# Decode attention of a small YOCO trunk: eight key places, a maximum in two parts, another ACT order, query copies on GpSimd

## Chip, core and metric

The program runs on one core of one Trainium2 chip. The metric is the device time of one execution in microseconds. The kernel before takes 1780.01 us (median of three runs, 1779.8 to 1782.85).

PE is the matmul engine, ACT ScalarE, DVE VectorE, POOL GpSimd, SP the engine whose queue issues the loads and stores of this stage.

## The reference, cut to what matters

One inference step: an mLSTM layer, a shared key and value projection, a differential attention layer and a final norm, for 1024 prompt rows and for 8 decode batches of 4 rows each. The change touches the attention of the decode batches. Each has 8 pages of 128 past rows in a paged cache (chosen by `page_table`) and its 4 new rows:

```python
k_past = cache_k[page_table].reshape((db, past_len) + cache_k.shape[2:])
v_past = cache_v[page_table].reshape((db, past_len) + cache_v.shape[2:])
...
for kp, mk in zip(k_parts, masks):
    s = jnp.einsum('bqhcd,bkhcd->bhcqk', q, kp).astype(F32) * ATTN_SCALE
...
p = jax.nn.softmax(jnp.concatenate(scores, axis=-1), axis=-1)
w = p[:, :, 0] - lam * p[:, :, 1]
o = jnp.einsum('bhqk,bkhe->bqhe', w[..., start:start + s_len].astype(vp.dtype), vp)
```

There are 8 heads with two key parts (c) of 64 numbers each, so a batch has 8 x 2 x 4 = 64 rows of scores over 1056 columns (1024 past, 32 new of which the mask leaves the batch's own). Everything is fp32; the kernel splits an operand into a high part (rounded for the matmul) and a low part (the remainder) and adds the products.

## The kernel before

The decode stage is `decode_phase`, between the prompt's attention and the last output projection. It runs over `DB` = 8 batches, software-pipelined: body b works on the keys of batch b and the values of batch b−1 (and on PE, ACT and SP on what is left of batch b−2). Bodies 0, 1, 8 and 9 are written out, bodies 2 to 7 are a loop on each engine. Each engine runs its own fixed list of steps in order and meets the others at semaphores:

```python
PE_ORDER = ("T0", "V4", "V5", "T1", "V6", "T2", "V7", "N", "T3", "S0", "W", "S1",
            "T4", "V0", "T5", "V1", "T6", "V2", "T7", "S2", "V3", "S3")
ACT_ORDER = ("K0", "V0", "E", "K1", "Q", "X", "V1", "K2", "V2", "K3", "V3", "O", "W",
             "K4", "V4", "K5", "R0", "V5", "K6", "V6", "K7", "R1", "V7", "R2")
DVE_ORDER = ("K0", "K1", "E", "K2", "K3", "W", "K4", "K5", "R0", "K6", "K7", "R1", "R2", "M")
```

The steps, with the lines they have in the profile:

- **T p** (PE, L2545): transposes key page p, in two halves u = 2p and 2p+1 of four heads each, into one of three PSUM banks used in turn. Half u+3 needs the bank that half u had (with W taking one turn in the middle), so it waits until u was read by DVE.
- **K p**: ACT copies the high part of both halves (L2378), DVE writes the low part (L2468, inputs: a PSUM bank and the high part in SBUF).
- **Q** (ACT, L2399): four copies of 64 rows put this batch's query parts into the zeroed `QZ`, which the scores use as weights.
- **S g** (PE, L2559): 16 matmuls of `QZ` with 256 columns of keys (288 for S3). **R r**: ACT copies the rows of the low query part (L2390), DVE adds them to the others in `SR` (L2477).
- **M** (DVE): mask on the last 32 columns (L2483), maximum over 1056 columns (L2484), scaling (L2485). **E**: exponentials with their sum on ACT (L2404), reciprocal and product `cf = rc * sgn` on DVE (L2489, L2490). **X** (ACT, L2409): scales the rows by `cf`.
- **W**: PE transposes the weights (L2569, L2571), DVE adds the two parts (L2495, L2497), ACT writes the high part (L2414, L2415), DVE the low part (L2503, L2505, all operands in SBUF).
- **V p**: ACT copies value page p to its high part (L2385), GpSimd subtracts to get the low part (L2357, "value low"), PE does four matmuls (L2582). There are four places for value pages `VB`, four for the high and four for the low parts; ACT's copy of page p waits until PE is done with page p−4 in `av`.
- **N** (PE): the new rows' values. **O** (ACT): copies the output to `AVS`, which SP stores.

SP issues the loads in one fixed order: key pages 4 to 7 of batch b in turn with value pages 4 to 7 of batch b−1, a store, then key pages 0 to 3 of batch b+1 in turn with value pages 0 to 3 of batch b. A key page waits until the page four before it was transposed (four places, `KB`), a value page until the low of the page four before it is done. Behind the last value pages SP loads the eight tiles of y rows that the next stage adds to (`X1`, a view of the rows' buffer `Y_ROWS`).

Of the kernel before, what the change touches and what calls it, by code (L numbers as in the profile page):

```python
# [24 lines left out]
P = 128  # L25
# [3 lines left out]
NT = 8  # L29
# [95 lines left out]
def trunk_step(  # L125
# [50 lines left out]
    with ctx:  # L176
# [2041 lines left out]
        def decode_phase():  # L2218
# [3 lines left out]
            ROWS = H * 2 * DS  # L2222
            KB = RAW[:, 0:4 * D].rearrange("p (s n) -> p s n", s=4)
            VB = take(4, D)
            SR, SX = take(TOK), take(TOK)
            AVS = take(D)
            WS = take(NB * TS)
            sgn, mx, nm, sm, rc, cf = (take(1) for _ in range(6))
            QZ = WH[:, 0:H * 136]
# [8 lines left out]
            d_in, d_avs, d_yr = sem("d_in"), sem("d_avs"), sem("d_yr")  # L2238
            k_ld = [sem(f"d_k{s}") for s in range(4)]
            v_ld = [sem(f"d_v{s}") for s in range(4)]  # L2240
# [53 lines left out]
            with nc.Block() as block:  # L2294
                @block.sync
                def _(sp):
                    for j, dst in enumerate((VB[0:TS, 2, :], VB[0:TS, 3, :], AVS[0:TS, :])):
                        sp.dma_start(dst, d_smB[:, j, :]).then_inc(d_in, 16)

                    def keys(b, p):  # L2300

                        wait(sp, tp, 2 * PAGES * b + 2 * (p - 3))
                        src = cache_k[page(sp, b * PAGES + p), :, :, :, :]
                        sp.dma_start(KB[:, p % 4, :], src.rearrange("a p h c d -> (a p) (h c d)"))\
                          .then_inc(k_ld[p % 4], 16)

                    def values(i, p):

                        wait(sp, vl, PAGES * i + p - 3)
                        src = cache_v[page(sp, i * PAGES + p), :, :, :]  # L2310
                        sp.dma_start(VB[:, p % 4, :], src.rearrange("a p h e -> (a p) (h e)"))\
                          .then_inc(v_ld[p % 4], 16)

                    def store(i):
                        sp.wait_ge(avc, i + 1)
                        sp.dma_start(d_av[bass.ds(i, 1), :, :].rearrange("a r n -> (a r) n"), AVS[0:64, :])\
                          .then_inc(d_avs, 16)

                    def body(b):
                        for p in range(4, PAGES):  # L2320
                            keys(b, p)
                            values(b - 1, p)
                        if has_rest(b):
                            store(b - 2)
                        for p in range(4):
                            keys(b + 1, p)
                            values(b, p)

                    for p in range(PAGES):
                        keys(0, p)  # L2330
                    for p in range(4):
                        keys(1, p)
                        if p == 2:
                            sp.wait_ge(pre, 1)
                        values(0, p)
                    body(1)
                    with sp.Fori(2, DB - 1) as b:
                        body(b)
                    for p in range(4, PAGES):
                        keys(DB - 1, p)  # L2340
                        values(DB - 2, p)
                    store(DB - 3)
                    for p in range(PAGES):
                        values(DB - 1, p)
                    store(DB - 2)
                    for t in range(NT):
                        sp.dma_start(X1[:, t, :], d_y[tok(t, P), :]).then_inc(d_yr, 16)
                    store(DB - 1)
                    sp.wait_ge(d_avs, 16 * DB)
                    sp.wait_ge(d_yr, 16 * NT)  # L2350

                @block.gpsimd
                def _(pool):
                    with pool.Fori(0, DB) as i:
                        for p in range(PAGES):
                            pool.wait_ge(vh, PAGES * i + p + 1)
                            nc.gpsimd.tensor_tensor(VL[p % 4], VB[:, p % 4, :], VH[p % 4].bitcast(F32), ALU.subtract)\  # L2357
                              .then_inc(vl, 1)

                @block.scalar  # L2360
                def _(act):
# [10 lines left out]
                    def body(b):  # L2372
# [8 lines left out]
                        def v_high(p):  # L2381
                            act.wait_ge(v_ld[p % 4], 16 * (2 * i + p // 4 + 1))

                            wait(act, av, PAGES * i + p - 3)
                            act.activation(VH[p % 4], VB[:, p % 4, :], ACT.Copy).then_inc(vh, 1)  # L2385

# [4 lines left out]

                        def queries():

                            wait(act, sc, 4 * b)
                            for part, q in ((0, QH), (64, QL)):
                                for c in range(2):
                                    rows = slice(DK * c, DK * c + DK)
                                    at = part + DS * c
                                    act.activation(QZ.rearrange("p (h r) -> p h r", r=136)[rows, :, at:at + DS],  # L2399
                                                   q[rows, :, bass.ds(b * DS, DS)].bitcast(F32), ACT.Copy).then_inc(qz, 1)  # L2400

                        def exponentials():
                            act.wait_ge(mxs, i + 1)
                            act.activation(SR[0:64, :], SR[0:64, :], ACT.Exp, scale=ATTN_SCALE, bias=nm[0:64, :],  # L2404
                                           accum_out=sm[0:64, :]).then_inc(exd, 1)
# [18 lines left out]
                        for step in ACT_ORDER:  # L2424
                            if step[0] == "K" and has_keys(b):
                                k_high(int(step[1]))
                            elif step[0] == "R" and has_keys(b):
                                low_rows(int(step[1]))
                            elif step == "Q" and has_keys(b):
                                queries()  # L2430
# [13 lines left out]
                def _(dve):  # L2444
# [16 lines left out]
                    def body(b):  # L2461
# [9 lines left out]
                        def add_rows(r):  # L2471
                            if r == 0 and has_weights(b):
# [35 lines left out]
                        for step in DVE_ORDER:  # L2508
# [4 lines left out]
                            elif step == "M" and has_keys(b):  # L2513
                                maximum()
                            elif step == "E" and has_weights(b):
                                shares()
# [5 lines left out]
                def _(pe):  # L2522
# [9 lines left out]
                    def body(b):  # L2532
                        i = b - 1

                        def turn(p):
                            pe.wait_ge(k_ld[p % 4], 16 * (2 * b + p // 4 + 1))
                            for j in range(2):
# [6 lines left out]
                                for h in range(4):  # L2544
                                    x = nc.tensor.transpose(T_BANK[u][:, h * P:(h + 1) * P],  # L2545
                                                            KB[:, p % 4, (4 * j + h) * P:(4 * j + h + 1) * P], ident)
                                x.then_inc(tp, 1)
# [101 lines left out]
```

## Time and profile before

| | us |
|---|---|
| median of three runs | 1780.01 |
| profiled execution | 1779.63 |
| its span, first to last instruction | 1777.8 |
| decode: from the first T0 (1409.70) to the next stage's first matmul (1659.80) | 250.1 |
| first batch, T0 to T0 | 20.75 |
| second batch | 28.70 |
| third to eighth batch, each | 27.83 to 27.91 |
| from the last S3's end of PE's eighth batch to the next stage | 33.5 |

Over the whole span PE is busy 94%, its weight loads 77%, DVE 54%, ACT 47% and GpSimd 25%. Those shares mix stages with different limits: the decode stage is 14% of the span, and only it contains what the change touches. In it the page's slices show DMA at 0.8 to 0.9 (nearly the only place in the program where it is), and a busy share of PE below that of the rest.

How to read the rows further down: a timeline row has its start (us from the span's start), its length, the engine, the line, output and inputs, how many merged instructions it stands for, and in brackets how long the engine had been idle ahead of it and who ended that. The ends of matmul records are modelled, so a record often overlaps the next start.

### The profile page before, as it was taken

To read this page: it belongs to the slowest core of one execution; us is meant where nothing else is said; L and a number is where in the kernel's file an instruction comes from. 1 tells how busy PE (TensorE), PEld (TensorE's weight loads), DVE (VectorE), ACT (ScalarE), POOL (GpSimd) and SP (SyncE) were. 2 spreads that over 40 slices of the span, in tenths; PEclk is the share of its full clock that TensorE was granted. 3 is DMA by queue.
4 is the path that set the end of the run, shared out by engine and by line. 5 is a ranking of instruction groups with operands and counts; after the bars stand their busy time and mean duration, and the time that the engine had idled before them with its cause. 6 is when DMAs were issued, how large, how long until landed. Compare 5 with 4: busy or idle time off the path is not lost. (4 is left out here: it accounts for less than half of the span.)

```text
span 1777.8 us, 30961 instructions
## 1 busy us (share of the span) xinstructions
PE 1665.1 (94%) x9247; PEld 1360.5 (77%) x9247; DVE 967.9 (54%) x2551; ACT 839.3 (47%) x1991; POOL 436.0 (25%) x866
## 2 busy tenths in 40 slices
PE   6999999999999979979999999999999689997798
PEld 5788888888888857768878878788788667775576
DVE  4454444544445343345776767767766455555343
ACT  5444443434445222343555545555544478876322
POOL 2122121221212210010122221221222147676201
PEclk9999999999999989989999999999998899998899
DMA  6212404033040113422121221111101388896713
GB/s 198 73 19 81 98 0 98 14 83 78 19 98 2 38 35 124 131 80 71 34 67 44 59 59 41 56 46 55 41 13 36 113 295 302 308 317 235 243 55 117
DMA packets 170406, 172.34 MB, mean 97 GB/s; under 512 B 13030, under 2 KB 140390, under 8 KB 170310
## 3 DMA queue, kind: packets, MB, share of 16 engines
q1 hardware_dynamic: 170310, 171.18, 31.9%
q8 instruction: 45, 0.74, 0.2%
q14 instruction: 51, 0.42, 0.1%
HBM read 142.24 MB, written 28.91 MB: 96 GB/s over the span
## 5 line engine op out<-in xcount | busy, mean ns | idle before, releaser
L1137 PE MATMUL PS<-WH,XH 128*128 128x512 f32 x512 | 212.7, 415 | 0.2 <-issue 0.2
L1137 PE MATMUL PS<-WH,XL 128*128 128x512 f32 x512 | 201.9, 394 | 0.0
L1137 PE MATMUL PS<-WL,XH 128*128 128x512 f32 x512 | 201.9, 394 | 0.0
L1867 ACT ACTIVATE WORK<-PD,WORK 128x896 f32<-128x896 f32 (+7 forms) x128 | 95.0, 743 | 62.1 <-DVE WORK L2034 57.3
L2113 PE MATMUL PS<-W,XH 128*128 128x512 f32 x384 | 123.8, 403 | 0.0
L1137 PEld LDWEIGHTS PS<-WH,XL 128*128 128x128 f32 x512 | 96.2, 188 | 22.9
L1137 PEld LDWEIGHTS PS<-WH,XH 128*128 128x128 f32 x512 | 96.8, 189 | 20.4 <-issue 0.6
L1137 PEld LDWEIGHTS PS<-WL,XH 128*128 128x128 f32 x512 | 96.8, 189 | 17.1
L1931 POOL TENSOR_SCALAR WORK<-WORK 128x1 f32<-128x1 f32 x64 | 19.9, 312 | 363.6 <-ACT WORK L1901 363.6
L2357 POOL TENSOR_TENSOR WL<-WORK,WH 128x1024 fp32r<-128x1024 f32 x32 | 76.2, 2383 | 94.2 <-ACT WH L2385 93.2
L730 POOL TENSOR_SCALAR WORK<-WORK 128x1 f32<-128x1 f32 (+1 forms) x72 | 13.8, 191 | 345.0 <-ACT WORK L581 345.0
L2033 DVE TENSOR_REDUCE WORK<-PD 128x1 f32<-128x896 f32 (+7 forms) x128 | 96.4, 753 | 2.2
L2113 PE MATMUL PS<-WH,XH 128*128 128x512 f32 (+2 forms) x224 | 86.5, 386 | 3.2 <-ACT WH L1832 3.2
L2468 DVE TENSOR_TENSOR XL<-PS,XH 128x512 fp32r<-128x512 f32 x96 | 63.5, 686 | 43.6 <-ACT XH L2378 41.3
L872 DVE SCALAR_TENSOR_TENSOR WORK<-PS,WORK 128x128 f32<-128x128 f32 (+1 forms) x72 | 20.1, 278 | 117.8 <-PE PS L1163 115.5
L2113 PE MATMUL PS<-WH,XL 128*128 128x512 f32 (+2 forms) x224 | 83.0, 370 | 0.0
L2113 PE MATMUL PS<-WL,XH 128*128 128x512 f32 (+2 forms) x224 | 82.8, 370 | 0.0
L2113 PEld LDWEIGHTS PS<-W,XH 128*128 128x128 f32 x384 | 68.8, 188 | 14.9 <-issue 1.4
L2195 PEld LDWEIGHTS PS<-RAW 128*128 128x128 f32 x576 | 75.1, 195 | 6.5 <-issue 1.4
L2545 PE MATMUL PS<-cst,RAW 128*128 128x128 f32 x384 | 58.3, 283 | 23.2 <-DVE XL L2468 18.8
L2357 POOL TENSOR_TENSOR WL<-WORK,VH 128x1024 fp32r<-128x1024 f32 x32 | 76.3, 2400 | 8.5 <-ACT VH L2385 8.5
L2195 PE MATMUL PS<-RAW 128*128 128x128 f32 x576 | 76.5, 279 | 1.3 <-DVE WORK L2000 1.3
(384 smaller groups left out, 4570.6 us busy)
## 6 DMA issues: line engine op xcount, KB each, us to landing
RAW<-in_cache_k SPq DMA_DIRECT2D x64, 512.0 KB, 5.1
WORK<-in_cache_v SPq DMA_DIRECT2D x64, 512.0 KB, 4.6
RAW<-in_w_in_a SPq DMA_DIRECT2D x40, 512.0 KB, 8.5
out<-WORK SPq DMA_DIRECT2D x16, 512.0 KB, 3.0
out<-RAW SPq DMA_DIRECT2D x16, 512.0 KB, 3.2
RAW<-in_w_in_b SPq DMA_DIRECT2D x60, 128.0 KB, 2.3
RAW<-in_w_kv SPq DMA_DIRECT2D x56, 128.0 KB, 2.2
YX<-in_x_prompt SPq DMA_DIRECT2D x8, 512.0 KB, 5.6
```

The source lines that it names most:

```text
L730: links.link(g_.tensor_scalar(var[0:n, b:b + 1], ssq[0:n, b:b + 1], 4.0 / P, 16 * EPS, ALU.mult, ALU.add))
L872: v.scalar_tensor_tensor(AT[0:n, t % 2, 0:n], B_S[0:n, 0:n], K_SCALE, EX[0:n, t % 2, 0:n], ALU.mult, ALU.mult).then_inc(at, 1)
L1137: last = nc.tensor.matmul(bank, x[:, k, tok(t, P)], wkvoz(w)[:, k, :], start=(k == i == 0), stop=(k == KT - 1 and i == 2))
L1867: act.activation(PR[:, c, 0:n], S[c][:, 0:n], ACT.Exp, scale=ATTN_SCALE, bias=nm[:, c:c + 1], accum_out=sm[:, c:c + 1]).then_inc(ex, 1)
L1931: links.link(g.tensor_scalar(var[:, b:b + 1], ssq[:, b:b + 1], 1.0 / P, EPS, ALU.mult, ALU.add))
L2033: links.link(v.tensor_reduce(mx[:, c:c + 1], S[c][:, 0:n], AX, ALU.max, negate=True))
L2113: last = nc.tensor.matmul(out, x[:, k, at(NT - 1 - s)], w[:, k, cols], start=(k == i == 0), stop=(k == KT - 1 and i == 2))
L2195: x = nc.tensor.matmul(B_O, WT[:, kb, :], V[:, kb, :], start=(kb == 0), stop=(kb == t))
L2357: nc.gpsimd.tensor_tensor(VL[p % 4], VB[:, p % 4, :], VH[p % 4].bitcast(F32), ALU.subtract)\
L2468: v.tensor_tensor(XL[cols], T_BANK[2 * p + j].rearrange("p (h t) -> p h t", h=4), XH[cols].bitcast(F32), ALU.subtract).then_inc(kl, 1)
L2545: x = nc.tensor.transpose(T_BANK[u][:, h * P:(h + 1) * P], KB[:, p % 4, (4 * j + h) * P:(4 * j + h + 1) * P], ident)
```

## The change

1. Key pages get eight places: pages 0 to 3 stay in `RAW`, pages 4 to 7 go to tiles 4 to 7 of the rows' buffer `X1`, which is empty in this stage. Key page p of batch b+1 is issued at the turn in SP's order at which page p of batch b has been transposed. All of batch 0's keys are issued at once. Tiles 0 to 3 of y are loaded ahead of the last value pages of batch 6, tiles 4 to 7 after the last transpose.
2. The maximum is taken in two parts: a new step P (DVE, between R1 and R2) reduces the first 768 columns to `mp`; M reduces the last 288, and the scaling takes the smaller of the two negated maxima.
3. ACT's list changes: V0 goes behind E and K1; V1, V2 and V3 each go behind the key copies that followed them (V3 also behind O and W); Q is taken out.
4. The four query copies become `queries` on GpSimd, ahead of the value lows of the same turn; GpSimd's loop runs over batches 1 to 7, with the first queries and the last lows outside.

```diff
-            KB = RAW[:, 0:4 * D].rearrange("p (s n) -> p s n", s=4)
+            key_page = lambda p: RAW[:, p * D:(p + 1) * D] if p < 4 else X1[:, p, :]
...
-            ACT_ORDER = ("K0", "V0", "E", "K1", "Q", "X", "V1", "K2", "V2", "K3", "V3", "O", "W",
+            ACT_ORDER = ("K0", "E", "K1", "V0", "X", "K2", "V1", "K3", "V2", "O", "W", "V3",
                          "K4", "V4", "K5", "R0", "V5", "K6", "V6", "K7", "R1", "V7", "R2")
-            DVE_ORDER = ("K0", "K1", "E", "K2", "K3", "W", "K4", "K5", "R0", "K6", "K7", "R1", "R2", "M")
+            DVE_ORDER = ("K0", "K1", "E", "K2", "K3", "W", "K4", "K5", "R0", "K6", "K7", "R1", "P", "R2", "M")
...
                     def keys(b, p):
 
-                        wait(sp, tp, 2 * PAGES * b + 2 * (p - 3))
+                        wait(sp, tp, 2 * PAGES * (b - 1) + 2 * (p + 1))
...
                     def body(b):
-                        for p in range(4, PAGES):
-                            keys(b, p)
-                            values(b - 1, p)
+                        for p in range(4):
+                            keys(b + 1, p)
+                            values(b - 1, p + 4)
                         if has_rest(b):
                             store(b - 2)
                         for p in range(4):
-                            keys(b + 1, p)
+                            keys(b + 1, p + 4)
                             values(b, p)
...
+                    def queries(b):
+
+                        wait(pool, sc, 4 * b)
+                        apart(pool)
+                        for part, q in ((0, QH), (64, QL)):
+                            for c in range(2):
+                                rows = slice(DK * c, DK * c + DK)
+                                at = part + DS * c
+                                nc.gpsimd.tensor_copy(QZ.rearrange("p (h r) -> p h r", r=136)[rows, :, at:at + DS],
+                                                      q[rows, :, bass.ds(b * DS, DS)].bitcast(F32)).then_inc(qz, 1)
+                        pool.wait_ge(qz, 4 * b + 4)
...
+                    queries(0)
+                    with pool.Fori(1, DB) as b:
+                        queries(b)
+                        lows(b - 1)
+                    lows(DB - 1)
...
+                        def part_maximum():
+                            dve.wait_ge(add, 3 * b + 2)
+                            if has_weights(b):
+                                dve.wait_ge(mxs, 2 * (i + 1))
+                            v.tensor_reduce(mp[0:64, :], SR[0:64, 0:3 * G], AX, ALU.max, negate=True).then_inc(mxs, 1)
...
-                            links.link(v.tensor_reduce(mx[0:64, :], SR[0:64, :], AX, ALU.max, negate=True))
-                            v.tensor_scalar(nm[0:64, :], mx[0:64, :], ATTN_SCALE, None, ALU.mult).then_inc(mxs, 1)
+                            links.link(v.tensor_reduce(mx[0:64, :], SR[0:64, 3 * G:TOK], AX, ALU.max, negate=True))
+                            dve.wait_ge(mxs, 2 * b + 1)
+                            v.tensor_scalar(nm[0:64, :], mx[0:64, :], mp[0:64, :], ATTN_SCALE, ALU.min, ALU.mult).then_inc(mxs, 1)
```

ACT in the second batch's body, from K0 to the weights, before: K0, V0 (1024 columns), E (1056), K1, the four query copies, X (1056), V1, K2, V2.

```order
L2378 ACTIVATE XH<-PS 128x4x128 x2
L2385 ACTIVATE WH<-WORK 128x1024
L2404 ACTIVATE WORK<-WORK 64x1056
L2378 ACTIVATE XH<-PD 128x4x128
L2378 ACTIVATE XH<-PS 128x4x128
L2399 ACTIVATE WH<-WH 64x8x4 x2
L2399 ACTIVATE WH<-QL 64x8x4 x2
L2409 ACTIVATE WORK<-WORK 64x1056
L2385 ACTIVATE WH<-WORK 128x1024
L2378 ACTIVATE XH<-PS 128x4x128
L2378 ACTIVATE XH<-PD 128x4x128
L2385 ACTIVATE VH<-WORK 128x1024
```

The same place on ACT after (L2402 are the key copies, L2409 the value copies, L2418 is E, L2423 X, L2428 the weights' high part):

```order
L2402 ACTIVATE XH<-PS 128x4x128 x2
L2418 ACTIVATE WORK<-WORK 64x1056
L2402 ACTIVATE XH<-PD 128x4x128
L2402 ACTIVATE XH<-PS 128x4x128
L2409 ACTIVATE WH<-WORK 128x1024
L2423 ACTIVATE WORK<-WORK 64x1056
L2402 ACTIVATE XH<-PS 128x4x128
L2402 ACTIVATE XH<-PD 128x4x128
L2409 ACTIVATE WH<-WORK 128x1024
L2402 ACTIVATE XH<-PS 128x4x128 x2
L2409 ACTIVATE VH<-WORK 128x1024
L2428 ACTIVATE WH<-WORK 128x8x32
```

K2 now stands directly behind X, and the value copies one place later each; the last of the four is behind the weights.

GpSimd in its loop after, from the query copies (L2364) to the first two value lows (L2371); before, the loop held the lows alone.

```order
L2364 COPY WH<-WH 64x8x4
L2364 ISA
L2364 COPY WH<-WH 64x8x4
L2364 ISA
L2364 COPY WH<-QL 64x8x4
L2364 ISA
L2364 COPY WH<-QL 64x8x4
L2366 REGISTER_ALU
L2370 ISA
L2371 TENSOR_TENSOR WL<-WORK,WH 128x1024
L2370 REGISTER_ALU
L2371 TENSOR_TENSOR WL<-WORK,WH 128x1024
```

Four copies were added in front of the eight lows of a turn, and nothing moved among the lows.

## Rows read from the trace of the kernel before

**Rows 1.** Stretches: bounds, length, busy PE PEld DVE ACT POOL, clock, DMA, GB/s.

```profile
1430.45:1459.15 28.70, 22.36 (x155) 18.96 (x154) 14.79 (x28) 21.16 (x36) 17.31 (x8) 0.94 0.80 284
1514.89:1542.72 27.83, 25.58 (x176) 20.04 (x174) 16.11 (x28) 22.16 (x38) 18.98 (x9) 1.00 0.90 315
```

**Rows 2.** Timeline of PE in one batch of the loop.

```profile
1518.94 0.66 PE L2545 MATMUL PS<-cst,RAW 128*128 128x128 f32 x4 [0.74 <-DVE XL L2468]
...
1524.72 0.66 PE L2545 MATMUL PS<-cst,RAW 128*128 128x128 f32 x4 [0.74 <-DVE XL L2468]
1527.19 0.71 PE L2569 MATMUL PD<-cst,WORK 64*128 64x64 f32 x8
...
1531.10 0.42 PE L2582 MATMUL PD<-WH 128*64 128x512 f32 x1 [0.18 <-issue]
...
1536.47 1.44 PE L2545 MATMUL PS<-cst,RAW 128*128 128x128 f32 x8 [0.31 <-DMA RAW<-in_cache_k]
```

**Rows 3.** Timeline of DVE in the same batch.

```profile
1515.53 0.45 DVE L2477 TENSOR_TENSOR WORK<-PD,WORK 64x288 f32<-64x288 f32 x1 [2.69 <-ACT WORK L2390]
...
1516.52 1.25 DVE L2484 TENSOR_REDUCE WORK<-WORK 64x1 f32<-64x1056 f32 x1
...
1518.20 1.29 DVE L2468 TENSOR_TENSOR XL<-PS,XH 128x512 fp32r<-128x512 f32 x2 [0.25 <-issue]
...
1521.15 0.15 DVE L2490 TENSOR_TENSOR WORK<-WORK 64x1 f32<-64x1 f32 x1
...
1529.41 1.49 DVE L2503 TENSOR_TENSOR WH<-WORK,WH 128x256 fp32r<-128x256 f32 x1 [0.60 <-ACT WH L2415]
1530.82 0.17 DVE L2505 TENSOR_TENSOR WH<-WORK,WH 32x32 fp32r<-32x32 f32 x1
...
1536.51 0.69 DVE L2468 TENSOR_TENSOR XL<-PS,XH 128x512 fp32r<-128x512 f32 x1 [0.80 <-ACT XH L2378]
```

**Rows 4.** Timeline of ACT in the same batch.

```profile
1520.13 0.47 ACT L2399 ACTIVATE WH<-WH 64x32 fp32r x2
...
1521.34 1.18 ACT L2409 ACTIVATE WORK<-WORK 64x1056 f32<-64x1056 f32 x1 [0.24 <-DVE WORK L2490]
1522.42 1.04 ACT L2385 ACTIVATE WH<-WORK 128x1024 fp32r<-128x1024 f32 x1
1523.37 0.57 ACT L2378 ACTIVATE XH<-PS 128x512 fp32r<-128x512 f32 x1
...
1524.32 1.05 ACT L2385 ACTIVATE VH<-WORK 128x1024 fp32r<-128x1024 f32 x1
```

**Rows 5.** Timeline of POOL in the same batch: value lows 0 to 3.

```profile
1518.02 2.39 POOL L2357 TENSOR_TENSOR WL<-WORK,WH 128x1024 fp32r<-128x1024 f32 x1 [1.58 <-ACT WH L2385]
1523.54 2.38 POOL L2357 TENSOR_TENSOR WL<-WORK,WH 128x1024 fp32r<-128x1024 f32 x1 [3.13 <-ACT WH L2385]
1525.88 4.74 POOL L2357 TENSOR_TENSOR WL<-WORK,VH 128x1024 fp32r<-128x1024 f32 x2
```

**Rows 6.** Timeline of DVE in the prompt's attention: a reduction of 384 columns.

```profile
1381.80 0.56 DVE L2033 TENSOR_REDUCE WORK<-PD 128x1 f32<-128x384 f32 x1
```

**Rows 7.** Timeline of POOL in the prompt's attention: a small operation with two inputs.

```profile
1395.63 0.46 POOL L1956 TENSOR_TENSOR WORK<-WORK 128x128 f32<-128x128 f32 x1
```

**Rows 8.** Timelines of PE and DVE in the second batch.

```profile
1439.98 0.66 PE L2545 MATMUL PS<-cst,RAW 128*128 128x128 f32 x4 [2.89 <-DVE XL L2468]
...
1446.15 0.43 DVE L2503 TENSOR_TENSOR WH<-WORK,WH 128x256 fp32r<-128x256 f32 x1 [0.60 <-ACT WH L2415]
```

**Rows 9.** Timeline of DVE after the last score: the eighth batch's weights.

```profile
1636.59 1.56 DVE L2503 TENSOR_TENSOR WH<-WORK,WH 128x256 fp32r<-128x256 f32 x1 [2.66 <-ACT WH L2415]
1638.07 2.32 DVE L2505 TENSOR_TENSOR WH<-WORK,WH 32x32 fp32r<-32x32 f32 x1
```

**Rows 10.** Timeline of SP (key page 7's issue) and landing times of value pages (L2311).

```profile
1530.51 0.34 SPq L2304 DMA_DIRECT2D RAW<-in_cache_k  x1
...
DMA to landing us min/median/max: 3.4/4.6/6.9
```

More of the change, by code:

```diff
@@ L2222, in decode_phase @@
             ROWS = H * 2 * DS
-            KB = RAW[:, 0:4 * D].rearrange("p (s n) -> p s n", s=4)
+            key_page = lambda p: RAW[:, p * D:(p + 1) * D] if p < 4 else X1[:, p, :]
             VB = take(4, D)
+            value_page = lambda p: VB[:, p % 4, :]
             SR, SX = take(TOK), take(TOK)
@@ L2227, in decode_phase @@
             WS = take(NB * TS)
-            sgn, mx, nm, sm, rc, cf = (take(1) for _ in range(6))
+            sgn, mx, mp, nm, sm, rc, cf = (take(1) for _ in range(7))
             QZ = WH[:, 0:H * 136]
@@ L2238, in decode_phase @@
             d_in, d_avs, d_yr = sem("d_in"), sem("d_avs"), sem("d_yr")
-            k_ld = [sem(f"d_k{s}") for s in range(4)]
+            k_ld = [sem(f"d_k{s}") for s in range(PAGES)]
             v_ld = [sem(f"d_v{s}") for s in range(4)]
@@ L2310, in values @@
                         src = cache_v[page(sp, i * PAGES + p), :, :, :]
[L2311 to L2312 removed]
+                        sp.dma_start(value_page(p), src.rearrange("a p h e -> (a p) (h e)")).then_inc(v_ld[p % 4], 16)
                     def store(i):
@@ L2331, in _ @@
                     for p in range(4):
-                        keys(1, p)
                         if p == 2:
@@ L2335, in _ @@
                         values(0, p)
+                    for p in range(PAGES):
+                        keys(1, p)
                     body(1)
@@ L2338, in _ @@
                         body(b)
+                    for t in range(4):
+                        sp.dma_start(X1[:, t, :], d_y[tok(t, P), :]).then_inc(d_yr, 16)
                     for p in range(4, PAGES):
-                        keys(DB - 1, p)
                         values(DB - 2, p)
@@ L2344, in _ @@
                         values(DB - 1, p)
+                    sp.wait_ge(tp, 2 * PAGES * DB)
+                    for t in range(4, NT):
+                        sp.dma_start(X1[:, t, :], d_y[tok(t, P), :]).then_inc(d_yr, 16)
                     store(DB - 2)
-                    for t in range(NT):
-                        sp.dma_start(X1[:, t, :], d_y[tok(t, P), :]).then_inc(d_yr, 16)
                     store(DB - 1)
@@ L2353, in _, with lows @@
                 def _(pool):
-                    with pool.Fori(0, DB) as i:
+                    def queries(b):
[8 more added lines that the diff above has]
+                        pool.wait_ge(qz, 4 * b + 4)
+                    def lows(i):
                         for p in range(PAGES):
                             pool.wait_ge(vh, PAGES * i + p + 1)
-                            nc.gpsimd.tensor_tensor(VL[p % 4], VB[:, p % 4, :], VH[p % 4].bitcast(F32), ALU.subtract)\
+                            nc.gpsimd.tensor_tensor(VL[p % 4], value_page(p), VH[p % 4].bitcast(F32), ALU.subtract)\
                               .then_inc(vl, 1)
+                        pool.wait_ge(vl, PAGES * i + PAGES)
+                    pool.wait_ge(pre2, 1)
+                    pool.wait_ge(ini, 2)
+                    pool.wait_ge(vn, 2)
+                    queries(0)
[3 more added lines that the diff above has]
+                    lows(DB - 1)
                 @block.scalar
@@ L2384, in v_high @@
                             wait(act, av, PAGES * i + p - 3)
-                            act.activation(VH[p % 4], VB[:, p % 4, :], ACT.Copy).then_inc(vh, 1)
+                            act.activation(VH[p % 4], value_page(p), ACT.Copy).then_inc(vh, 1)
                         def low_rows(r):
@@ L2390, in low_rows @@
                             act.activation(SX[0:64, at:at + n], bank[64:128, 0:n], ACT.Copy).then_inc(slo, 1)
[L2392 to L2400, printed above, removed]
                         def exponentials():
-                            act.wait_ge(mxs, i + 1)
+                            act.wait_ge(mxs, 2 * (i + 1))
                             act.activation(SR[0:64, :], SR[0:64, :], ACT.Exp, scale=ATTN_SCALE, bias=nm[0:64, :],
@@ L2428, in body @@
                                 low_rows(int(step[1]))
-                            elif step == "Q" and has_keys(b):
-                                queries()
                             elif step == "E" and has_weights(b):
@@ L2514, in body @@
                                 maximum()
+                            elif step == "P" and has_keys(b):
+                                part_maximum()
                             elif step == "E" and has_weights(b):
@@ L2535, in turn @@
                         def turn(p):
-                            pe.wait_ge(k_ld[p % 4], 16 * (2 * b + p // 4 + 1))
+                            pe.wait_ge(k_ld[p], 16 * (b + 1))
                             for j in range(2):
```

5 lines of the change are left out of this document (2 added, 3 removed).

## Prediction, made before the kernel ran

> **What bounds the kernel now.** I read the table of stretches first [rows 1]. The decode stage handles eight batches, one after the other. From the third to the eighth a batch takes 27.83 to 27.84 us, from one T0 on PE to the next; one of the six equal rows stands there. PE is busy 25.58 us of it, DVE 16.11, ACT 22.16 and GpSimd 18.98, at a granted clock of 1.00, with DMA at 0.90. So no engine is full, and the 27.83 is a ring of waits. The PE timeline shows where PE stands still [rows 2]: 0.74 before the second half of T1, 0.74 before the second half of T3 (both for DVE's low halves of keys), 0.18 before V0, and 0.31 before T7 for a key page. Recorded ends overlap the next start, so the two 0.74 are about 0.9 from start to start. What ends these waits is read from DVE and ACT [rows 3, 4]:
>
> - T1's second half waits for the first key low of the batch, which starts at 1518.20. DVE is held until then by the maximum over 1056 columns, 1.25 us from 1516.52.
> - T3's second half waits for the key low of page 2, whose high half ACT starts at 1523.37. Ahead of it on ACT stand the query copies (1520.13), X (1521.34) and value page 1 (1522.42).
> - V0 waits for the weights' low halves on DVE (L2503, L2505). L2503 takes 1.49 us from 1529.41 and ends at 1530.90, just after GpSimd's pair of value lows that began at 1525.88 ends at 1530.62 [rows 5]. In the second batch, with GpSimd idle, the same instruction takes 0.43 [rows 8]. At the end of the stage L2505 takes 2.32 behind such a low [rows 9]. So a DVE operation with both inputs in SBUF stands still while a value low runs; key lows (one input in PSUM) don't.
>
> The Trainium skill, "SBUF — State Buffer", section "Who interferes with whom", calls this a lock on a port pair shared by the two engines, kept for a whole instruction and given to whichever starts first; 0.43 against 1.49 agrees.
>
> **Maximum in two parts.** The part over 768 columns runs between R1 and R2, where DVE waits for the last score anyway (the addition of R2 starts at 1515.53 after a wait of 2.69, in the same timeline [rows 3]), and it needs about 1 us: hidden. On the path 288 columns are left. Two reductions give the slope, 1.25 us for 1056 columns and 0.56 for 384 [rows 3, 6]: 0.69/672, so 288 cost about 0.46 and the path loses 0.79. Bounds: 0.69 (if it costs what 384 columns do) and 0.9 (proportional). Key low, exponentials (E) and X start 0.79 earlier. The 0.9 before T1's second half shrinks to about 0.1.
>
> **ACT order and query copies.** Now K2 follows X at once. From X's start, K2 comes 1.08 later (as value page 1 does now, 1522.42 − 1521.34), and T3's second half 1.35 after K2's start (1524.72 − 1523.37): 2.43 after X. X moves from 1521.34 to 1520.55, so that half starts at 1522.98 instead of 1524.72, **1.74 earlier**. PE's own work allows it: without both waits it would be there at about 1523.0 (1524.72 less twice 0.9, plus the 0.1 left at T1). W and everything behind it move along. The page-0 value copy (1.06) now stands between K1 and X, where the queries (0.97) stood, so it costs X nothing.
>
> The four query copies go to GpSimd. Nearest rows: 0.24 each on ACT (half of 0.47 [rows 4]), 0.46 for a larger operation with two inputs on GpSimd [rows 7]; so 1.0 to 1.8 us a batch, and I take 1.4. They lie between value low 7, which ends at 1516.44 (1.58 before 1518.02 [rows 5]), and value low 0, which now starts near 1520.5: 4 us of cover, and S0 needs them only later. Cost nothing; past 4 us each further us would delay value low 0, which PE needs only after W.
>
> **From W to V0.** Today 3.91 us (1527.19 to 1531.10 [rows 2]). Everything is now counted from X. The copy of value page 1 follows K2's two (0.95, 1523.37 to 1524.32), lasts 1.04, and its low begins 0.08 behind it: X + 1.08 + 0.95 + 1.04 + 0.08 = X + 3.15. Lows follow each other by 2.34 and last 2.38 [rows 5], so low 2 ends at X + 7.87. W is at X + 2.43 + 2.47 = X + 4.90 (1527.19 − 1524.72), and L2503 is ready 2.22 behind W as today, at X + 7.12. It is held by low 2 and ends at X + 8.15 (0.28 after the low, as now). L2505 starts 0.08 ahead of that end, at X + 8.07, and ends at X + 8.24. S1 and T4 on PE end about 3.5 behind W, at X + 8.4, so V0 comes about 3.57 behind W with no wait: **0.34 saved**. This needs L2505 to be there before value low 3. With V3 behind W on ACT, the copy of page 3 starts about 0.13 before L2503 is ready (ACT's records overlap by 0.1), lasts 1.05, and its low asks 0.08 later, at X + 8.12. The margin is 0.05 us, and it is the weakest step.
>
> **Eight key places.** The 0.31 at T7 is worth nothing by itself: T7's second half waits for the low of page 6, which runs from 1536.51 to 1537.20 [rows 3], whatever the page does. But page 7 is requested only at 1530.51 [rows 10], behind a value request. With T7 two us earlier, its lateness would eat the gain. The eight places are cover, not a term. On SP the keys keep their turns between value requests. The rows of y that are now loaded ahead of the last value pages take the turns of keys that no longer exist: nothing.
>
> **The value pages** are asked for when a low frees a place. Value low 0 moves from 1518.02 to about 1520.5, while the copies of pages 4 to 7 are wanted 2 us earlier. A value page lands 4.6 us after its issue in the median and 6.9 at most [rows 10]; by the walk page 6 keeps about 0.4 us of slack. Some of the gain may stay here.
>
> **The sum.** Per batch 1.74 + 0.34 = 2.08 by starts; by PE's recorded waits 0.74 + 0.74 + 0.18 = 1.66. I take 1.9, nearer to the starts, with something left for pages: six batches, 11.4. The second batch has no first wait to W's lock, but a recorded 2.89 us before T3's second half [rows 8]; K2 without value page 1 (0.95) and with the shorter maximum (0.79) saves 1.8. The first batch loses the query copies ahead of K2: 0.9. After the last score, E now precedes value low 0, so value low 1 queues behind it and L2505 waits behind one low fewer: L2505, at 1640.39 today [rows 9], comes about 2.2 earlier (bounds 0.4 and 2.3; the nearer is the walk, since L2503 comes 0.28 before the low that would decide it). Together 11.4 + 1.8 + 0.9 + 2.2 = 16.3. The profiled execution took 1779.63 (span 1777.8), 0.4 below the median of 1780.01: 1763.3 against it, **1763.7** as a median.
>
> **The rivals.**
>
> (a) *Value low 3 beats L2505.* If GpSimd asks first, L2505 ends with low 3, at about X + 10.52 instead of X + 8.24: 2.28 us later in each of seven batches, 16.0 in all, and everything is given back: about 1780. For it: a margin of 0.05, and at the end of the stage a waiting low did go ahead of L2505. Against: there it had long been waiting. 0.25.
>
> (b) *GpSimd wins both close races* (the case on the slow side). Value low 0 now starts right beside L2490 (cf = rc·sgn, two SBUF inputs), which releases X. L2490 starts 0.10 us before it: today 1521.15, while value page 0 copied in the queries' place would end at 1521.17 and its low start at 1521.25. If GpSimd's hold starts over 0.1 us ahead of its record, L2490 waits a whole low, 2.36, and L2505 loses as well: 4.64 × 7 = 32.5, so 1763.7 + 32.5 = 1796. Against: ACT needs still more time between K1 and the copy, which favours DVE. 0.12. L2490 alone lost gives 1763.7 + 16.5 = 1780, 0.05.
>
> By the Trainium skill's rule of that section, first come first served, neither race is lost and the forecast stands; no row here shows so close a pair.
>
> (c) *Pages of values are late.* If they land in 6 us instead of 4.6, V5 and V6 on ACT start about 1 us late, and half of each batch's gain goes: 1763.7 + 7 = 1771. 0.08. Here the order does what it says, but the ring closes through SP.
>
> **How the numbers follow.** My forecast has 0.50. Against no change, 0.2% (3.6 us, about what a measurement of this kernel can tell) is the bound. Faster: 0.50, (c) 0.08, and 0.05 of (a), whose time could end a little below, 0.63 in all. Same: 0.17 of (a) and the 0.05 of L2490 alone, 0.22. Slower: (b) 0.12 and 0.03 of (a), 0.15. The forecast's own range is 1759 to 1769: 2.08 in each batch and 2.3 at the end give 1762.5, and a second batch at full clock (0.94 now [rows 1]) about 1.3 less; 1.66, 0.4 and late pages give 1767 to 1769. The range reaches to (a), 1759 to 1781, and leaves out (b) and the tails.
>
> **What would show it.** Right: a batch of 25.8 to 26.2 us between T0s; no wait over 0.2 before the second halves of T1 and T3; the second weights' low (today L2505) at 0.17 us and the product behind the reciprocal (today L2490) at 0.15; GpSimd's query copies over before value low 0. Wrong: the second weights' low at over 2 us (a), that product as well (b), ACT's value copies waiting for DMA (c), or a batch that stays at 27.8 with PE waiting somewhere else.

## The result and the profile after

The changed kernel takes **1764.65 us** (median of four runs, 1763.86 to 1766.19) against 1780.6 for the kernel before, timed beside it: ratio 0.9909, 95% interval 0.9892 to 0.9927. The prediction was 1763.7. The profiled execution took 1764.56, 15.07 less than that of before. Decode itself became 16.7 us shorter (233.4 us from the first T0, at 1411.21, to the next stage's first matmul; 250.1 before). Of that, 1.5 us were lost again ahead of it: decode's first T0 came at 1409.70 before, behind stages that no part of the change touches.

The stretches of the kernel after (bounds, length, busy PE PEld DVE ACT POOL, clock, DMA, GB/s): first batch, second batch, one batch of the loop, and from the end of the loop to the next stage.

```profile
1411.21:1431.07 19.86, 18.06 (x128) 16.19 (x129) 12.32 (x19) 9.94 (x18) 0.64 (x4) 0.91 1.01 395
1431.07:1458.08 27.01, 22.34 (x156) 19.03 (x154) 15.02 (x29) 20.38 (x32) 18.18 (x12) 0.94 0.78 273
1509.78:1535.65 25.87, 25.03 (x175) 20.15 (x174) 15.91 (x29) 21.34 (x34) 19.94 (x13) 1.00 0.91 336
1613.29:1644.65 31.36, 17.18 (x68) 8.58 (x65) 5.33 (x10) 13.33 (x18) 20.42 (x9) 0.76 0.52 183
```

Against [rows 1] a loop batch fell from 27.83 to 25.87 while PE's busy time hardly moved (25.58 to 25.03): waits went, work did not. PE's timeline in that batch (start, length, engine, line, operation; in brackets the idle time ahead and who ended it):

```profile
1513.14 0.66 PE L2566 MATMUL PS<-cst,RAW 128*128 128x128 f32 x4
...
1517.51 1.16 PE L2566 MATMUL PS<-cst,RAW 128*128 128x128 f32 x8
...
1520.50 0.71 PE L2590 MATMUL PD<-cst,WORK 64*128 64x64 f32 x8
...
1523.98 0.47 PE L2603 MATMUL PD<-WH 128*64 128x512 f32 x1
...
1530.18 0.66 PE L2566 MATMUL PS<-cst,Y_ROWS 128*128 128x128 f32 x4 [0.66 <-DVE XL L2480]
```

The second halves of T1 (1513.14) and T3 (inside the group at 1517.51) have no wait; [rows 2] had 0.74 at each. W is the row at 1520.50, V0 the one at 1523.98. The wait for a key page at T7 is gone too, but T7's second half (1530.18) waits 0.66 for page 6's key low. DVE in the same batch (L2502 is the shorter reduction, L2504 the scaling, L2480 key lows, L2509 `cf`, L2522 and L2524 the weights' lows):

```profile
1511.42 0.45 DVE L2502 TENSOR_REDUCE WORK<-WORK 64x1 f32<-64x288 f32 x1
1511.99 0.20 DVE L2504 TENSOR_SCALAR WORK<-WORK 64x1 f32<-64x1 f32 x1
1512.39 1.29 DVE L2480 TENSOR_TENSOR XL<-PS,XH 128x512 fp32r<-128x512 f32 x2 [0.20 <-issue]
...
1515.40 0.15 DVE L2509 TENSOR_TENSOR WORK<-WORK 64x1 f32<-64x1 f32 x1
...
1522.71 1.07 DVE L2522 TENSOR_TENSOR WH<-WORK,WH 128x256 fp32r<-128x256 f32 x1 [0.60 <-ACT WH L2429]
1523.71 0.17 DVE L2524 TENSOR_TENSOR WH<-WORK,WH 32x32 fp32r<-32x32 f32 x1
```

GpSimd: the first two rows are the query copies (two merged in each), the other four value lows 0 to 3.

```profile
1511.90 0.47 POOL L2364 CAST WH<-WH 64x32 fp32r x2 [0.55 <-POOL WL L2371]
1512.42 0.47 POOL L2364 CAST WH<-QL 64x32 fp32r x2
1515.49 2.39 POOL L2371 TENSOR_TENSOR WL<-WORK,WH 128x1024 fp32r<-128x1024 f32 x1 [2.60 <-ACT WH L2409]
1518.75 2.39 POOL L2371 TENSOR_TENSOR WL<-WORK,WH 128x1024 fp32r<-128x1024 f32 x1 [0.87 <-ACT WH L2409]
1521.10 2.41 POOL L2371 TENSOR_TENSOR WL<-WORK,VH 128x1024 fp32r<-128x1024 f32 x1
1523.71 2.44 POOL L2371 TENSOR_TENSOR WL<-WORK,VH 128x1024 fp32r<-128x1024 f32 x1 [0.20 <-ACT VH L2409]
```

The queries are over at 1512.89, 2.6 us before value low 0. L2522 stands still until value low 2 ends (1523.51), as [rows 3] showed for the same step. L2524 and value low 3 are recorded at the same hundredth, 1523.71, and L2524 takes 0.17. On ACT, X starts at 1515.59:

```profile
1515.59 1.18 ACT L2423 ACTIVATE WORK<-WORK 64x1056 f32<-64x1056 f32 x1 [0.17 <-DVE WORK L2509]
```

### The profile page after: what moved, and what is told of

The parts are those of the page before. It is cut to its first block and busy times, and to the rows that moved or that the text cites. A ratio compares the mean times of both kernels' runs of the same rounds, so it can differ in the third digit from the quotient of the medians.

```text
span 1762.7 us, 31001 instructions
## 1 busy us (share of the span) xinstructions
PE 1664.2 (94%) x9247; PEld 1362.8 (77%) x9247; DVE 965.6 (55%) x2559; ACT 832.8 (47%) x1959; POOL 442.9 (25%) x898
## 5 line engine op out<-in xcount | busy, mean ns | idle before, releaser
L2480 DVE TENSOR_TENSOR XL<-PS,XH 128x512 fp32r<-128x512 f32 x96 | 63.3, 687 | 39.1 <-ACT XH L2402 38.1
L2371 POOL TENSOR_TENSOR WL<-WORK,WH 128x1024 fp32r<-128x1024 f32 x32 | 76.2, 2385 | 32.0 <-ACT WH L2409 31.3
L2371 POOL TENSOR_TENSOR WL<-WORK,VH 128x1024 fp32r<-128x1024 f32 x32 | 76.9, 2406 | 11.5 <-ACT VH L2409 11.5
L668 ACT ACTIVATE WORK<-PS 128x512 f32<-128x512 f32 x64 | 38.2, 598 | 84.5 <-PE PS L1137 84.5
```

Source lines behind the costliest of these rows:

```text
L668: act.activation(PJS[:, t % 2, :, 0:2 * P], PJ[(3 + t) % 2].rearrange("p (a c) -> p a c", a=2), ACT.Copy).then_inc(ev, 1)
L2371: nc.gpsimd.tensor_tensor(VL[p % 4], value_page(p), VH[p % 4].bitcast(F32), ALU.subtract)\
L2480: v.tensor_tensor(XL[cols], T_BANK[2 * p + j].rearrange("p (h t) -> p h t", h=4), XH[cols].bitcast(F32), ALU.subtract).then_inc(kl, 1)
```

## The experiments

Decode lengths (first T0 to the next stage's first matmul) come from each profiled execution; a loop batch is the mean of five, from W to W. Ratios are to the kernel before, timed beside each, with the 95% interval. The other stages move by several us from run to run, so the decode columns are the cleaner measure. They are not free of PE's granted clock, whose mean over a stretch mixes its two levels, 1.2 and 2.4 GHz (a mean of 1.00 is the upper one throughout). In the loop it was 1.00, but for one of the five batches at 0.94, some 0.9 us longer, in each of three runs: four places, V3 ahead of O and W, and the tiny operation. Outside the loop it differed from run to run. The same kernel (R0 behind K6, both runs) took 26.55 us in its second batch at 0.87 and 25.44 at 1.00; PE's waits just ahead were alike (1.21 and 0.59), so why the clock fell in one of them is open.

| kernel | median us | ratio | decode | loop batch |
|---|---|---|---|---|
| before | 1780.01 | | 250.1 | 27.83 |
| changed | 1764.65 | 0.9909 [0.9892, 0.9927] | 233.4 | 25.87 |
| changed, again | 1765.88 | 0.9907 [0.9891, 0.9924] | 233.0 | 25.87 |
| eight places alone | 1781.38 | 0.9995 [0.9984, 1.0007] | 250.0 | 27.83 |
| changed, four places | 1777.27 | 0.9969 [0.9952, 0.9985] | 246.4 | 27.82 |
| changed, one maximum | 1770.89 | 0.9926 [0.9905, 0.9946] | 243.1 | 26.53 |
| changed, queries on ACT | 1771.6 | 0.9939 [0.9920, 0.9958] | 239.1 | 26.60 |
| changed, old ACT order | 1781.71 | 0.9995 [0.9986, 1.0005] | 250.2 | 27.67 |
| changed, V3 ahead of O and W | 1783.69 | 1.0007 [0.9996, 1.0017] | 252.5 | 28.16 |
| changed, tiny operation between the lows | 1778.55 | 0.9982 [0.9969, 0.9995] | 249.2 | 28.22 |
| changed, K6 ahead of V5 and R0 | 1762.19 | 0.9896 [0.9877, 0.9915] | 233.8 | 25.83 |
| changed, R0 behind K6 | 1761.34 | 0.9884 [0.9868, 0.9901] | 230.0 | 25.48 |
| the same, again | 1758.43 | 0.9869 [0.9848, 0.9889] | 228.8 | 25.51 |
| the same and V3 behind K4 | 1766.16 | 0.9914 [0.9898, 0.9929] | 236.5 | 26.41 |

**Eight places alone**, on the kernel before:

```diff
-            KB = RAW[:, 0:4 * D].rearrange("p (s n) -> p s n", s=4)
+            key_page = lambda p: RAW[:, p * D:(p + 1) * D] if p < 4 else X1[:, p, :]
...
-                        wait(sp, tp, 2 * PAGES * b + 2 * (p - 3))
+                        wait(sp, tp, 2 * PAGES * (b - 1) + 2 * (p + 1))
```

> The kernel before with the eight key places and SP's new order alone (one maximum, the old ACT order, queries on ACT). My account: the recorded 0.31 us wait for a key page before T7 goes away, but a batch stays at 27.8 us, since T7's second half waits for the low of page 6 anyway; the time stays within 0.1% of the kernel before (1780.6). Rival, the places as the source of a gain by themselves: 0.31 x 7 = 2.2 us off or more, a batch of 27.5 and about 1778.

No difference, and PE's timeline says why. The wait for page 7 is gone from T7, and its second half waits for DVE in its place:

```profile
1512.52 0.66 PE L2547 MATMUL PS<-cst,Y_ROWS 128*128 128x128 f32 x4 [0.66 <-DVE XL L2470]
```

**Changed, with four places** and the old order of loads (the reverse of the diff above):

> The changed kernel with four key places and the old order of loads; the rest as changed. My account: the places are cover for the gain. Page 7 is issued about 16 us after T0 (behind value page 6's request) and lands about 5.4 later, at 21.3, while T7 wants it at 19.1; T7's second half comes at about 21.8 instead of 20.4, so a batch is about 1.3 us longer (27.0 to 27.3) and the time about 1764.65 + 7 x 1.3 = 1774, with PE waiting for key pages by DMA before T6 and T7. Rival, the places do nothing: 1764.65 and 25.87.

12.6 us over the changed kernel, more than expected. PE waits for key pages, at other steps from batch to batch: 2.2 to 2.5 us in five of the six loop batches and 1.2 in the last. The batches lie between 27.4 and 28.0, and the one at the lower clock at 28.7:

```profile
1507.36 0.32 PE L2563 MATMUL PS<-cst,RAW 128*128 128x128 f32 x1 [2.40 <-DMA RAW<-in_cache_k]
...
1531.87 0.65 PE L2563 MATMUL PS<-cst,RAW 128*128 128x128 f32 x4 [1.46 <-DMA RAW<-in_cache_k]
```

So the places are worth nothing alone, and most of the gain hangs on them.

**Changed, with one maximum:**

```diff
-            DVE_ORDER = ("K0", "K1", "E", "K2", "K3", "W", "K4", "K5", "R0", "K6", "K7", "R1", "P", "R2", "M")
+            DVE_ORDER = ("K0", "K1", "E", "K2", "K3", "W", "K4", "K5", "R0", "K6", "K7", "R1", "R2", "M")
...
-                            links.link(v.tensor_reduce(mx[0:64, :], SR[0:64, 3 * G:TOK], AX, ALU.max, negate=True))
...
+                            links.link(v.tensor_reduce(mx[0:64, :], SR[0:64, :], AX, ALU.max, negate=True))
```

> The changed kernel with the maximum over 1056 columns in one piece (no step P). My account: it lies on the path from the last score to E, so E, X and all behind them come 0.8 us later; a batch is 26.6 to 26.7 us and the time about 1764.65 + 7 x 0.8 = 1770. Rival: it is hidden behind ACT's other work, 25.9 and 1765.

As expected: 0.66 us more in a batch, and the wait of [rows 2] before T1's second half is back with its 0.74:

```profile
1520.16 0.33 PE L2565 MATMUL PS<-cst,RAW 128*128 128x128 f32 x1 [0.74 <-DVE XL L2480]
```

The 243.1 in the table is more than the maximum's share: of the 9.7 us over the changed kernel 3.4 lie in the second batch, which ran at a lower clock here (0.78 against 0.94) with PE busy 26.04 us of it against 22.34:

```profile
1432.65:1463.01 30.36, 26.04 (x156) 22.41 (x155) 14.81 (x28) 20.39 (x32) 18.18 (x12) 0.78 0.69 236
```

**Changed, with the queries back on ACT** (GpSimd's copies taken out):

```diff
-            ACT_ORDER = ("K0", "E", "K1", "V0", "X", "K2", "V1", "K3", "V2", "O", "W", "V3",
+            ACT_ORDER = ("K0", "E", "K1", "Q", "V0", "X", "K2", "V1", "K3", "V2", "O", "W", "V3",
```

> The changed kernel with the four query copies back on ACT, between K1 and the copy of value page 0; GpSimd does value lows alone. My account: the copies push the copy of value page 0 and with it X by 0.69 us (1516.28 instead of 1515.59 in the fifth batch's terms), so a batch is about 26.6 us, the first batch loses 0.9, and the time is about 1764.65 + 7 x 0.69 + 0.9 = 1770.4. Rival, the copies on GpSimd are themselves in the way there (they hold the port at the maximum's steps): then taking them away gives some of that back and the time stays at 1765 to 1767.

As expected: 0.73 more in a batch. X and K2 come later, and T3's second half waits again:

```profile
1520.57 0.33 PE L2561 MATMUL PS<-cst,RAW 128*128 128x128 f32 x1 [0.58 <-DVE XL L2475]
```

**Changed, with ACT's old order** (without Q):

```diff
-            ACT_ORDER = ("K0", "E", "K1", "V0", "X", "K2", "V1", "K3", "V2", "O", "W", "V3",
+            ACT_ORDER = ("K0", "V0", "E", "K1", "X", "V1", "K2", "V2", "K3", "V3", "O", "W",
```

> The changed kernel with ACT's steps in the order before, without Q: K0 V0 E K1 X V1 K2 V2 K3 V3 O W; eight places, two-part maximum and queries on GpSimd stay. My account: V0 delays E by about 0.4 us, V1 ahead of K2 delays T3's second half by 0.95 more, and the weights' low is held by value low 3 as before the change (0.34): together 1.7 a batch, 27.5 us, and the time about 1764.65 + 7 x 1.7 = 1776.5. Rival (Q and the maximum carry the gain, the order little): 0.4 a batch, about 1767.5.

A miss in the total, 1781.71 for 1776.5. A loop batch comes out near the expected 27.5, with all but 0.16 of its gain lost; the rest lies in the second batch (2.2 us more, at a clock of 0.88 for 0.94) and in the tail (3.8), which the estimate counted together as one batch more. ACT's timeline (value page 0's copy, then E) and DVE's (the scaling, done at 1548.83):

```profile
1548.41 1.07 ACT L2409 ACTIVATE WH<-WORK 128x1024 fp32r<-128x1024 f32 x1 [0.27 <-PE PD L2603]
1549.38 1.16 ACT L2418 ACTIVATE WORK<-WORK 64x1056 f32<-64x1056 f32 x1
```

```profile
1548.63 0.20 DVE L2504 TENSOR_SCALAR WORK<-WORK 64x1 f32<-64x1 f32 x1
```

The maximum is ready at 1548.83, but E starts at 1549.38, behind V0, which had to wait for PE's products. In the kernel before V0 had ended just as the longer maximum did. So the shorter maximum brings E forward only with V0 out of its way, and K2 then still stands behind V1.

**Changed, with V3 ahead of O and W on ACT**, so that GpSimd asks for value low 3 early:

```diff
-            ACT_ORDER = ("K0", "E", "K1", "V0", "X", "K2", "V1", "K3", "V2", "O", "W", "V3",
+            ACT_ORDER = ("K0", "E", "K1", "V0", "X", "K2", "V1", "K3", "V2", "V3", "O", "W",
```

> The changed kernel with one step of ACT moved: V3 stands ahead of O and W again. My account (the port): value low 3 is then already waiting on GpSimd when value low 2 ends, so it goes ahead of the second weights' low (0.17 us now), which is held for a whole low, about 2.3 us, in six batches of the loop; V0 comes 2.2 later, a batch is about 28.1 us and the time about 1764.65 + 7 x 2.2 = 1780. Rival (no such hold between two lows; only ACT's order counts): the weights' high part starts 0.26 later behind V3, a batch is 26.1 and the time about 1766.5.

The whole gain is gone. DVE's timeline, and GpSimd's with value lows 2 and 3 back to back:

```profile
1521.68 0.85 DVE L2522 TENSOR_TENSOR WH<-WORK,WH 128x256 fp32r<-128x256 f32 x1 [0.81 <-ACT WH L2429]
1522.45 2.33 DVE L2524 TENSOR_TENSOR WH<-WORK,WH 32x32 fp32r<-32x32 f32 x1
```

```profile
1519.85 4.89 POOL L2371 TENSOR_TENSOR WL<-WORK,VH 128x1024 fp32r<-128x1024 f32 x2
```

L2524 takes 2.32 or 2.33 in all six loop batches: a low that already waits goes ahead of DVE's next operation.

**Changed, with one tiny DVE operation more** between the two lows of the weights, to move the close race alone:

```diff
+                            v.reciprocal(rc[0:64, :], sm[0:64, :])
                             v.tensor_tensor(WTS[0:TS, PAGES, TS:2 * TS], ws[0:TS, PAGES, :],
```

> The changed kernel with one tiny DVE operation more (the reciprocal of 64x1 once again, 0.14 to 0.18 us, one input) between the two weights' lows L2522 and L2524. In the changed kernel the recorded start of value low 3 on GpSimd and that of L2524 lie within 0.02 us of each other in every loop batch, and L2524 took 0.17. If the two race for a shared port and the first to ask is served for a whole instruction (theory): L2524 now asks some 0.17 us behind value low 3, takes 2.2 us instead of 0.17, a batch lasts about 28 us as in the kernel with V3 ahead of O and W, and the total is about 1780. If DVE wins because a short operation behind another of DVE is let through, whoever came first (rival): L2524 stays at 0.17, a batch at 25.9 to 26.05 us, and the total within 1.5 us of the changed kernel.

The theory holds. DVE's and GpSimd's timelines (L2525 is the second weights' low here):

```profile
1525.97 1.06 DVE L2522 TENSOR_TENSOR WH<-WORK,WH 128x256 fp32r<-128x256 f32 x1 [0.60 <-ACT WH L2429]
1526.95 0.15 DVE L2524 RECIPROCAL WORK<-WORK 64x1 f32<-64x1 f32 x1
1527.03 2.32 DVE L2525 TENSOR_TENSOR WH<-WORK,WH 32x32 fp32r<-32x32 f32 x1
```

```profile
1526.96 2.34 POOL L2371 TENSOR_TENSOR WL<-WORK,VH 128x1024 fp32r<-128x1024 f32 x1 [0.21 <-ACT VH L2409]
```

The second low now starts 0.07 behind value low 3 (0.06 to 0.10 in the six loop batches), takes 2.3 and with it the gain. In the eight traces of kernels without this edit that keep V3 between W and K4, the two starts lay within 0.02 of each other in 49 batches (all the loop's and one ahead of it), and DVE's operation took 0.17 in all of them. Whether a tie goes to DVE, or GpSimd asks a little later than its record says, is not shown.

**K6 earlier.** The wait that was left, T7's second half for page 6's low, was attacked in two ways on ACT (and R0 behind K6 on DVE in both). First K6 ahead of V5 and R0:

```diff
-                         "K4", "V4", "K5", "R0", "V5", "K6", "V6", "K7", "R1", "V7", "R2")
-            DVE_ORDER = ("K0", "K1", "E", "K2", "K3", "W", "K4", "K5", "R0", "K6", "K7", "R1", "P", "R2", "M")
+                         "K4", "V4", "K5", "K6", "V5", "R0", "V6", "K7", "R1", "V7", "R2")
+            DVE_ORDER = ("K0", "K1", "E", "K2", "K3", "W", "K4", "K5", "K6", "R0", "K7", "R1", "P", "R2", "M")
```

> The changed kernel with K6 ahead of V5 and R0 on ACT, and K6 ahead of R0 on DVE. In the changed kernel PE's one long wait left in a batch is 0.66 us before T7's second half, for the low of page 6, whose high half ACT starts at 1528.80 behind R0 and V5. My account: with K6 at about 1527.4 that wait goes, a batch is 25.2 us and the time about 1764.65 - 7 x 0.66 = 1760. Rival: the copy of value page 5 comes a microsecond later, its low and the next value pages with it, and the wait turns up again at V6, S3 or a value page: 25.7 to 26, no gain.

Short of what was expected: 25.6 to 25.7 in five of six batches, 26.44 in one. T7's wait is gone, but PE now waits 0.62 for page 7's low before S3, and in the long batch a value page was 1.41 late on ACT:

```profile
1528.87 0.40 PE L2580 MATMUL PD<-XH,WH 128*128 128x288 f32 x1 [0.62 <-DVE XL L2480]
```

```profile
1477.64 1.06 ACT L2409 ACTIVATE VH<-WORK 128x1024 fp32r<-128x1024 f32 x1 [1.41 <-DMA WORK<-in_cache_v]
```

Then only R0 behind K6 (on DVE as in the diff above):

```diff
-                         "K4", "V4", "K5", "R0", "V5", "K6", "V6", "K7", "R1", "V7", "R2")
+                         "K4", "V4", "K5", "V5", "K6", "R0", "V6", "K7", "R1", "V7", "R2")
```

> The same idea in a smaller step: only R0 goes behind K6 on ACT and DVE, V5 keeps its place ahead of K6. My account: K6 starts 0.5 us earlier, so the 0.66 before T7's second half shrinks to about 0.16; a batch is 25.4 us and the time about 1764.65 - 7 x 0.5 = 1761. Rival: V6 waits for its value page already (0.16 us for DMA in the fifth batch) and PE's gain is given back there or at S3: 25.7 or more.

As expected: 25.48 in a batch and 1761.34 in all. This kernel and the changed one were then run again beside each other:

> The changed kernel once more, on the same chip as the run with R0 behind K6 below, for a direct comparison. Both theories: as before, 1764.65 within 1.5 us, a batch of 25.87 us from one T0 to the next.

> The changed kernel with R0 moved behind K6 on ACT and DVE (V5, K6, R0 on ACT; K6, R0 on DVE), once more beside it. If the 0.66 us wait before T7's second half is the last thing that costs the loop (theory): the batches again 25.3 to 25.7 us against 25.87, some 0.4 us in each of six batches and at most 0.6 elsewhere, so 2 to 3.5 us under the changed kernel. If the 3.3 us between the two medians so far came from the chips' other stages (rival): within 1 us of it.

**This version beats both kernels**: 1758.43 beside 1765.88 for the changed one, decode 4.2 us shorter. In the loop it gains 0.36 to 0.39 a batch, as expected. The 7.5 between the medians is more than the expected 2 to 3.5. Of the 4.2 in decode 2.7 lie in the loop and 1.4 in the second batch, which ran at a clock of 1.00 here and of 0.94 in the changed kernel; the remaining 3.3 between the medians lie in other stages and weren't taken apart.

Last, the same with V3 behind K4, to take the race away:

```diff
-            ACT_ORDER = ("K0", "E", "K1", "V0", "X", "K2", "V1", "K3", "V2", "O", "W", "V3",
-                         "K4", "V4", "K5", "V5", "K6", "R0", "V6", "K7", "R1", "V7", "R2")
+            ACT_ORDER = ("K0", "E", "K1", "V0", "X", "K2", "V1", "K3", "V2", "O", "W", "K4",
+                         "V3", "V4", "K5", "V5", "K6", "R0", "V6", "K7", "R1", "V7", "R2")
```

> The changed kernel with R0 behind K6 (as in the two runs above) and V3 behind K4 on ACT, so that value low 3 asks some 2.2 us later and no longer within 0.02 us of L2524. If the close race costs nothing as long as DVE has it (theory): L2524 stays at 0.17, W to V0 at 3.5 us, and the batches as without this edit, 25.3 to 25.7 us; total 1757 to 1762. What speaks against (rival): value page 7 waits for the place that value low 3 frees, which now comes free at some 1528.3 instead of 1526.2 on the changed kernel's clock, lands 5.1 us later at 1533.4 and is copied at 1533.7; with any delay of the transfer V7 waits up to 1 us on ACT, and a batch lasts 26 to 26.5, the total 1762 to 1767.

The rival holds: value low 3 now comes 2.2 us behind L2524, but value page 7 comes late, and ACT waits for it in five of the six loop batches (0.94 to 1.29):

```profile
1504.66 1.06 ACT L2409 ACTIVATE VH<-WORK 128x1024 fp32r<-128x1024 f32 x1 [1.05 <-DMA WORK<-in_cache_v]
```

## Why the prediction was right, step by step

**The sum.** Predicted 0.9 + 1.8 + 11.4 + 2.2 = 16.3; measured by the stretches 0.89 (first batch), 1.69 (second), 11.9 (six batches: 2.08 once, 1.96 five times) and 2.17 (tail), together 16.6. (The third batch of the kernel before took 27.90, not 27.83, and the second batch's 1.8 is 0.95 + 0.79 = 1.74 rounded up; neither matters.) A loop batch gave 1.96 for the 1.9 taken, and that is in part luck: the 1.9 left 0.18 of the 2.08 for late value pages, which cost a batch next to nothing, while the maximum fell short by 0.16. That the median came within 1 us of the forecast is luck too, since the stages ahead of decode moved by 1.5.

**The maximum** was mis-sized. The reduction came out as worked out (0.45; the slope gave 0.46), but X comes 5.81 behind T0 after 6.45: 0.64, not 0.79. The reduction is 0.80 shorter, but the scaling starts 0.12 behind its end for 0.03, and E 0.24 behind the scaling's start for 0.18, as the scaling with a second scalar takes 0.20 for 0.14. The first half of the batch (T0 to W) gave 12.30 − 10.72 = 1.58 instead of 1.74.

**The walk from X** held to 0.1 us: value low 1 at X + 3.16 (3.15 predicted), W at 4.91 (4.90), the end of value low 2 at 7.92 (7.87), L2522 ready at 7.12 (7.12), L2524 at 8.12 (8.07), value low 3 at 8.12 (8.12). W to V0 took 3.48 for 3.91 and saved 0.43, more than the 0.34 of the sum. Behind V0 a batch is 0.05 longer than before, so 1.58 + 0.43 − 0.05 = 1.96.

**The close races.** L2509 stands 0.09 ahead of value low 0 (0.10 predicted) and takes 0.15: won. The margin of L2524, 0.05 by the walk, is 0.00 in the record. That DVE won was the least sure step, and the tiny operation shows that rival (a) was a real mechanism with the price put on it: 28.06 for 25.87 in most batches, 1778.55 in all (1780 predicted).

**The tail.** As walked, L2522 now starts ahead of the low that decides, and L2524 alone pays for it, one low earlier than in [rows 9]; DVE's timeline there, and GpSimd's from that low on:

```profile
1622.47 0.51 DVE L2522 TENSOR_TENSOR WH<-WORK,WH 128x256 fp32r<-128x256 f32 x1 [1.61 <-ACT WH L2429]
1622.91 2.31 DVE L2524 TENSOR_TENSOR WH<-WORK,WH 32x32 fp32r<-32x32 f32 x1
```

```profile
1622.66 4.85 POOL L2371 TENSOR_TENSOR WL<-WORK,VH 128x1024 fp32r<-128x1024 f32 x2
```

**Query copies** were over-priced (about 1 us for 1.4), which costs nothing, since they are hidden either way. **Key places**: "cover, not a term" is confirmed from both sides (0.9995 alone; 12.6 us without them). **Value pages**: ACT waits 0.16 to 0.17 for page 6 in two of the six loop batches, so its slack of 0.4 was used up there. The profile's list of DMA issues (output and input, queue, count, KB each, median us to landing) shows value pages landing later, 5.1 for 4.6 in [rows 10].

```profile
WORK<-in_cache_v SPq DMA_DIRECT2D x64, 512.0 KB, 5.1
...
RAW<-in_cache_k SPq DMA_DIRECT2D x32, 512.0 KB, 5.2
Y_ROWS<-in_cache_k SPq DMA_DIRECT2D x32, 512.0 KB, 5.5
```

**What the working missed** is how the parts hang together. It credited the shorter maximum with X's move by itself; the old ACT order shows that V0 had to leave its place ahead of E first. Undoing parts one at a time costs a loop batch at clock 1.00 0.66 (maximum), 0.73 (queries), 1.80 (ACT order) and about 1.7 us (places): 4.9 in all for a change that gains 1.96. (By the medians, which hold the clock and the other stages too, it is 6, 7, 17 and 13 of 16.) They are links of one chain, not terms that add.

## What to carry to other kernels

In a ring of waits, ask of each part which of the others it needs: an edit that measures nothing alone (here the places) can be what the rest stands on, so undo parts from the finished version as well as trying them alone. Where DVE operations with both inputs in SBUF meet long GpSimd operations, walk both from a common start to a few hundredths, and treat a margin under 0.1 us as a step that any small edit can turn. Moving a copy away from such a race also moves the place that it frees: check when the transfer waiting for that place must land.

## What the runs showed of the hardware

- Starts recorded within 0.02 us of each other went to DVE in 49 of 49 batches; with DVE's 0.06 to 0.10 behind, GpSimd went first in 6 of 6. The lengths tell it too: value low 3 takes 2.42 to 2.46 where L2524 goes first and 2.34 or 2.35 where it goes first itself; the DVE operation takes 0.17 or 2.3.
- A waiting GpSimd operation gets in between two DVE operations that stand directly behind each other (0.85, then 2.33, with V3 early).
- GpSimd copies 64x8x4 in about 0.24 us each, as fast as ACT's copies of [rows 4].
- Half a megabyte of a page lands in 5.1 to 5.5 us in the median after the change (before: 4.6 for value pages, 5.1 for key pages); the DMA engines are busy 0.91 of a loop batch (0.90 before). A transfer that had 0.4 us of slack on paper was late in two of six batches.
- The same kernel's second batch took 26.55 us at a granted clock of 0.87 and 25.44 at 1.00, with PE busy 23.09 and 21.02 of it.
